# Choosing experts with wider operations, and expert weights in 8 KB pieces

## The chip, the cores and the metric

The kernel runs as one program on one core of a Trainium2 chip. The metric is device time in microseconds (us), the median of three runs. Engines: PE multiplies matrices, DVE and ACT work element by element, POOL (GpSimd) issues the indirect DMAs, SP issues all other DMAs.

## The reference

Two transformer blocks over 512 tokens of 1024 features, all in f32. The change touches only the mixture of experts in the first block. Each token goes to 2 of 32 experts, both from one group of 8:

```
lg = xs @ wr_g + br_g;  pg = softmax(lg);  ptop, gsel = top_k(pg, 1)
le = (xs @ wr_e + br_e) of the chosen group;  lv, esel = top_k(le, 2)
we = softmax(lv) * ptop;  gate = one_hot(gsel) x (we on esel)      # [S, 32]
h = silu(xs @ w_gate[e]) * (xs @ w_up[e]) * gate[:, e];  y = sum over e of h @ w_down[e]
```

An expert has w_gate and w_up of 1024x256 and w_down of 256x1024: three times 1 MB.

## The kernel before

The program is a row of stages. In a stage each engine has its own instruction list, held together by semaphores; a stage ends when all engines are through, and its POOL list begins by clearing the semaphores of the stage before (line 161). `c.settle()` is such a stage with nothing in it but the clearing. Three parts matter here.

**The choice** (`choose`, line 745) works on logits of [128 tokens, 4 row blocks, 36]. DVE runs one chain of small operations, each waiting for the one before (`run`): it finds the best group, masks the experts of the other groups (lines 823 to 828, once per row block), marks the two best experts (`mr`, line 833), and splits the marks into first and second choice (`sel`, `whom`). From `mr`, PE counts how many earlier tokens chose each expert (`ahead`) and how many in all (`total`): 14 matmuls of 32 columns. DVE turns the counts into places (`where`), PE multiplies `where` by `whom` into a list of up to 64 token numbers per expert (line 785), DVE stores it as `table`, and POOL gathers the tokens of experts 0 and 1 by indirect DMA. SP writes the largest count to DRAM. Before the stage ends, the weights of experts 0 and 1 are on their way (`c.to_fetch`, issued by SP as the stage begins).

**Between**: `c.settle()`, then every engine loads the largest count from DRAM into a register and branches; with at most 64 tokens per expert it takes `experts_by_token`.

**The experts** (`experts_by_token`, line 988). Three slots hold raw weights (`wgu`, `wd`); for expert j SP waits until slot j-3 is used up, then issues gate, up and down. The two first are one 256-column half each of `wgu[:, slot, k, 0:512]`. ACT rounds `wgu` in four parts to `w_hi` (line 1130), DVE takes the rest as `w_lo` (line 1171). In one period PE does in this order: gate and up of expert j (lines 1082, 1083: 16 matmuls), the transposes of the tokens of expert j+1 (line 1071, 8), down of expert j-1 (line 1103, 8 passes) and the sums of expert j (line 1091, 8 passes). An f32 matmul shows as two passes in the trace. The token rows `xg` are [64 tokens, 1024 features]; a transpose turns 128 features into partitions, and is the operand that PE loads.

Of the kernel before, what the change touches and what calls it, by code (L numbers as in the profile page):

```python
# [15 lines left out]
F32 = mybir.dt.float32  # L16
# [6 lines left out]
P = 128  # L23
# [721 lines left out]
def choose(c, lg, pair_gates, e, taken, table, most, x_dram, first):  # L745
# [5 lines left out]
    with ExitStack() as ctx:  # L751
        gl, le = c.sb(ctx, "group", [P, NT, 16]), c.sb(ctx, "expert", [P, NT, B])
        top, want, oh, ex = (c.sb(ctx, x, [P, NT, w]) for x, w in (("top", 8), ("want", 8), ("oh", 16), ("ex", 4)))
        mr, s1 = c.sb(ctx, "mr", [P, NT, B]), c.sb(ctx, "first", [P, NT, B])
# [4 lines left out]
        ps = c.ps(ctx, "lists", [P, 512])  # L759
        to_exp, exps, chain, picked, counted, listed, placed, stored = (  # L760
            c.sem(x) for x in ("to_exp", "exps", "dve", "picked", "counted", "listed", "placed", "stored"))
        ahead, total = ps[:, 0:NT * NE].rearrange("p (i e) -> p i e", e=NE), ps[:, NT * NE:NT * NE + NE]
        lists = ps[0:CAP, 256:256 + 2 * NE].rearrange("p (w e) -> p w e", w=2)
        xg, gi, xg_in, indexed = first
        with c.stage() as block:
            @block.sync
            def _(sp):
                sp.wait_ge(placed, 2)
                sp.dma_start(most, most_u[0:1, :]).then_inc(stored, 16)
                sp.wait_ge(stored, 16)  # L770

            @block.tensor
            def _(pe):
                pe.wait_ge(picked, 1)
                for i in range(NT):
                    for j in range(i + 1):
                        pe.matmul(ahead[:, i, :], c.const("before" if j == i else "ones"), mr[:, j, 0:NE],
                                  start=(j == 0), stop=(j == i))
                for i in range(NT):
                    mm = pe.matmul(total, c.const("ones"), mr[:, i, 0:NE], start=(i == 0), stop=(i == NT - 1))  # L780
                mm.then_inc(counted, 1)
                pe.wait_ge(placed, 1)
                for r in range(2):
                    for i in range(NT):
                        mm = pe.matmul(ps[0:CAP, 256:256 + 2 * NE], where[:, r, i, :], whom[:, r, i].rearrange("p w e -> p (w e)"),
                                       start=(r == 0 and i == 0), stop=(r == 1 and i == NT - 1))
                mm.then_inc(listed, 1)
# [9 lines left out]
            @block.gpsimd  # L797
            def _(pool):
                for u in range(2):
                    pool.wait_ge(indexed, u + 1)  # L800
                    pool.indirect_dma_start(out=xg[:, u, :], out_offset=None, in_=x_dram,
                                            in_offset=bass.IndirectOffsetOnAxis(ap=gi[:, u, :], axis=0),
                                            bounds_check=S - 1, oob_is_err=False).then_inc(xg_in[u], 16)

            @block.vector
            def _(dve):
                run = Chain(dve, chain)
                for u in range(2):
                    run(nc.vector.memset(xg[:, u, :], 0.0))
                run(nc.vector.memset(gl[:], NEG))  # L810
# [10 lines left out]
                dve.sem_inc(to_exp, 1)  # L821
                run(nc.vector.tensor_scalar(oh[:, :, 4:8], oh[:, :, 0:4], 1.0, -NEG, ALU.subtract, ALU.mult))
                for i in range(NT):
                    grouped = le[:, i, 0:NE].rearrange("p (g e) -> p g e", e=8)
                    run(nc.vector.tensor_tensor(grouped, lg[:, i, 4:36].rearrange("p (g e) -> p g e", e=8),
                                                oh[:, i, 0:4].unsqueeze(2).broadcast_to([P, 4, 8]), ALU.mult))
                    run(nc.vector.tensor_tensor(grouped, grouped, oh[:, i, 4:8].unsqueeze(2).broadcast_to([P, 4, 8]), ALU.add))
# [5 lines left out]
                run(nc.vector.tensor_scalar(mr[:], mr[:], -NEG / 2, None, ALU.is_ge))  # L833
                dve.sem_inc(picked, 1)
                run(nc.vector.tensor_tensor(e, le[:], top[:, :, 0:1].broadcast_to([P, NT, B]), ALU.subtract))
                run(nc.vector.tensor_tensor(st[:, :, 0:1], top[:, :, 1:2], top[:, :, 0:1], ALU.subtract))
                dve.sem_inc(to_exp, 1)
                run(nc.vector.memset(want[:], 2 * NEG))
# [3 lines left out]
                run(nc.vector.tensor_scalar(sel[:, 0], s1[:, :, 0:NE], -NEG / 2, None, ALU.is_ge))  # L842
                run(nc.vector.tensor_tensor(sel[:, 1], mr[:, :, 0:NE], sel[:, 0], ALU.subtract))
                pairs = c.const("pairs").rearrange("p (r i) -> p r i", r=2)
# [8 lines left out]
                for r in range(2):  # L853
                    for i in range(NT):
                        run(nc.vector.tensor_scalar(where[:, r, i, :], c.const("column"), place[:, r, i:i + 1], None, ALU.is_equal))
                run(nc.vector.tensor_reduce(cnt[:, 0], total, AX.X, ALU.max))
                dve.sem_inc(placed, 1)
                nc.vector.tensor_copy(most_u[:], cnt[:, 0]).then_inc(placed, 1)
                dve.wait_ge(listed, 1)
# [8 lines left out]
                run(nc.vector.tensor_tensor(pair_gates[:, :, 1:2], st[:, :, 1:2], st[:, :, 4:5], ALU.mult))  # L868
                run(nc.vector.tensor_tensor(taken, mr[:], st[:, :, 4:5].broadcast_to([P, NT, B]), ALU.mult))

# [32 lines left out]
def experts(c, x_t, y, gates, w_gate, w_up, w_down, wgu, wd):  # L903
# [3 lines left out]
    with ExitStack() as ctx:  # L907
        wg, wu = (wgu[:, n].rearrange("p k j -> p (k j)").rearrange("p (u k j) -> p u k j", u=2, k=KT) for n in range(2))
        gt = c.sb(ctx, "gt", [P, 2, S])
# [78 lines left out]
def experts_by_token(c, table, x_dram, y_dram, w_gate, w_up, w_down, room_yg, small, wgu, wd, gu_in, d_in, first):  # L988

    nc, U32 = c.nc, mybir.dt.uint32
    SLOTS, PARTS = EXPERT_SLOTS, 4
    xg, gi, xg_in, _ = first
    with ExitStack() as ctx:
# [13 lines left out]
        def part(t, p):  # L1010
            return t[:, 2 * p:2 * p + 2, :]

        with c.stage() as block:
            @block.sync
            def _(sp):
                for j in range(EARLY, NE):
                    s = j % SLOTS
                    if j >= SLOTS:
                        sp.wait_ge(w_split, PARTS * (j - SLOTS) + PARTS)
                    for dst, src in ((wgu[:, s, :, 0:HID], w_gate), (wgu[:, s, :, HID:], w_up)):  # L1020
                        sp.dma_start(dst, src[j].rearrange("(k p) n -> p k n", p=P)).then_inc(gu_in[s], 16)
                    if j >= SLOTS:
# [42 lines left out]
            def _(pe):  # L1065
                def turn_x(j):
                    pe.wait_ge(xg_in[j % 2], 16 * (j // 2) + 16)
                    if j:
                        pe.wait_ge(x_split, j)
                    for k in range(KT):  # L1070
                        mm = pe.transpose(rows_ps[:, k, :], xg[:, j % 2, k * P:(k + 1) * P], c.const("ident", CAP)[:, 0:CAP])
                    mm.then_inc(tx, 1)
# [45 lines left out]
            def _(act):  # L1118
# [6 lines left out]
                def w_round(j, p):  # L1125
                    if j < NE:
                        act.wait_ge(gu_in[j % SLOTS], 32 * (j // SLOTS) + 32)
                        if j:
                            act.wait_ge(used, PARTS * (j - 1) + p + 1)
                        nc.scalar.copy(part(w_hi, p), part(wgu[:, j % SLOTS], p)).then_inc(w_rounded, 1)  # L1130

# [30 lines left out]
            def _(dve):  # L1162
# [1676 lines left out]
def first_block(c, a, y_t, x_rows, lbs, pair, dram):  # L2839
# [4 lines left out]
    with ExitStack() as outer:  # L2844
# [593 lines left out]
```

## Time and profile before

| | us |
|---|---|
| median of the runs | 2459.65 (2458.9 to 2464.27) |
| the profiled execution | 2462.61 |
| its span, first to last instruction | 2460.8 |
| the choice, first to last gather issue | 767.6 to 793.9 |
| the experts, first transpose to last down | 798.7 to 1118.1 |

The rows of the trace give the start of a piece in us from the span's start, its length, engine, line, operation and operands. "x8" says that eight equal instructions stand together; square brackets hold the idle time before it and what ended that.

### The profile page before, as it was taken

The numbers are of one execution on the slowest core, as the hardware profiler recorded it, in microseconds if no ns is written. First come the engines' busy times: TensorE is split into PE (matmuls) and PEld (weight loads), VectorE is DVE, ScalarE is ACT, GpSimd is POOL, SyncE is SP. The second block draws the span as 40 slices with busy tenths as digits, with TensorE's granted clock in tenths as the row PEclk, the third lists the DMA queues.
The fourth block names the chain that finished last, engine by engine and source line by source line (L and its number), as shares of the span: only waits on it lengthen the run. The fifth ranks groups of instructions, "written<-read, shape, count | busy, mean of one in ns | idle before, by whom it ended". The sixth has DMA issues, their size and how long they took to land. (4 is left out here: it accounts for less than half of the span.)

```text
span 2460.8 us, 30153 instructions
## 1 busy us (share of the span) xinstructions
PE 2199.7 (89%) x11250; PEld 1658.7 (67%) x11250; DVE 1359.9 (55%) x2399; ACT 897.2 (36%) x1538; POOL 104.7 (4%) x151
## 2 busy tenths in 40 slices
PE   6898998899995999992799989999979998899997
PEld 4687765566775555551677768888757766788886
DVE  2643447766445655553345585974444456778544
ACT  3420233123232666654333342332333334233323
POOL 0000002100000222220000000000000000000000
PEclk8885999999996999996899999999989999999999
DMA  5221322222324999984332122323413221132313
GB/s 163 86 74 40 105 72 65 68 82 65 106 86 142 323 354 346 345 294 178 97 109 57 57 78 76 105 86 107 142 65 115 79 61 65 57 128 78 101 54 111
DMA packets 276334, 296.46 MB, mean 120 GB/s; under 512 B 48861, under 2 KB 248621, under 8 KB 276153
## 3 DMA queue, kind: packets, MB, share of 16 engines
q1 hardware_dynamic: 271066, 286.09, 36.0%
q0 software_dynamic: 5120, 8.40, 1.1%
q8 instruction: 92, 1.51, 0.2%
q14 instruction: 56, 0.46, 0.1%
HBM read 283.12 MB, written 22.07 MB: 124 GB/s over the span
## 5 line engine op out<-in xcount | busy, mean ns | idle before, releaser
L1551 PE MATMUL acc<-x_hi,w_hi 128*128 128x512 f32 x1432 | 579.9, 405 | 20.3 <-DVE w_lo L1502 16.9
L1552 PE MATMUL acc<-x_lo,w_hi 128*128 128x512 f32 x1432 | 566.7, 396 | 0.0
L1553 PE MATMUL acc<-x_hi,w_lo 128*128 128x512 f32 x1432 | 566.2, 395 | 0.0
L1472 ACT CAST w_hi<-raw 128x1024 fp32r<-128x1024 f32 x179 | 186.9, 1045 | 622.5 <-PE acc L1553 587.2
L1502 DVE TENSOR_TENSOR w_lo<-raw,w_hi 128x1024 fp32r<-128x1024 f32 x174 | 212.8, 1224 | 292.8 <-ACT w_hi L1472 289.5
L1551 PEld LDWEIGHTS acc<-x_hi,w_hi 128*128 128x128 f32 x1432 | 274.5, 192 | 84.6 <-DVE w_lo L1502 18.0
L1553 PEld LDWEIGHTS acc<-x_hi,w_lo 128*128 128x128 f32 x1432 | 273.5, 191 | 60.5
L1552 PEld LDWEIGHTS acc<-x_lo,w_hi 128*128 128x128 f32 x1432 | 274.5, 192 | 58.0 <-issue 2.0
L1171 DVE TENSOR_TENSOR w_lo<-wgu,w_hi 128x1024 fp32r<-128x1024 f32 x128 | 150.9, 1220 | 126.9 <-ACT w_hi L1130 126.9
L1130 ACT CAST w_hi<-wgu 128x1024 fp32r<-128x1024 f32 x128 | 127.9, 1045 | 110.1 <-DMA wgu<-in_moe_w_up 104.8
L1082 PE MATMUL ps<-w_hi,xs 128*128 128x512 f32 x256 | 106.2, 415 | 16.7 <-DVE xs L1165 13.7
L1103 PE MATMUL ps<-wd,y 128*64 128x512 f32 x256 | 116.7, 598 | 0.7 <-DVE y L1187 0.7
L1083 PE MATMUL ps<-w_lo,xs 128*128 128x512 f32 x256 | 102.6, 401 | 0.0
L1689 ACT ACTIVATE probs<-scores,stat 128x256 f32<-128x256 f32 (+3 forms) x96 | 51.8, 540 | 127.0 <-DVE stat L1651 126.8
L1511 DVE SCALAR_TENSOR_TENSOR sg<-sg,br 128x512 f32<-128x512 f32 x112 | 76.4, 682 | 34.9 <-PE br L1740 28.2
L2286 DVE SCALAR_TENSOR_TENSOR y_t<-pad,w,y_t 128x512 f32<-128x512 f32 x120 | 90.1, 751 | 3.4
L1698 ACT COPY probs_t<-t_ps 128x256 f32<-128x256 f32 (+3 forms) x96 | 39.1, 407 | 132.0 <-PE t_ps L1612 132.0
L1738 PE MATMUL br<-y_hi,b_hi 128*128 128x512 f32 x176 | 70.8, 403 | 17.1 <-DVE b_lo L1730 16.9
L1551 PE MATMUL acc<-x_hi,lead_hi 128*128 128x512 f32 x184 | 76.5, 416 | 1.3 <-PEq L157 1.0
L1483 ACT ACTIVATE sg<-acc 128x512 f32<-128x512 f32 x112 | 66.2, 591 | 30.2 <-PE acc L1553 30.2
L1552 PE MATMUL acc<-x_lo,lead_hi 128*128 128x512 f32 x184 | 73.9, 402 | 0.0
L1553 PE MATMUL acc<-x_hi,lead_lo 128*128 128x512 f32 x184 | 73.6, 400 | 0.0
(553 smaller groups left out, 3315.6 us busy)
## 6 DMA issues: line engine op xcount, KB each, us to landing
raw<-in_w_in SPq DMA_DIRECT2D x60, 1024.0 KB, 5.4
raw<-in_w_gate SPq DMA_DIRECT2D x40, 1024.0 KB, 5.5
wgu<-in_moe_w_gate SPq DMA_DIRECT2D x32, 1024.0 KB, 11.4
wgu<-in_moe_w_up SPq DMA_DIRECT2D x32, 1024.0 KB, 14.9
wd<-in_moe_w_down SPq DMA_DIRECT2D x32, 1024.0 KB, 9.4
raw_b<-in_w_branch SPq DMA_DIRECT2D x56, 256.0 KB, 2.7
room<-in_w_out SPq DMA_DIRECT2D x3, 2048.0 KB, 8.2
y_t<-in_w_out SPq DMA_DIRECT2D x3, 2048.0 KB, 10.5
```

The costliest lines, as they stand in the source:

```text
L1082: pe.matmul(ps[:, 0, :], xs[:, u, k, :], w_hi[:, k, :], start=(k == 0), stop=False)
L1083: mm = pe.matmul(ps[:, 0, :], xs[:, u, k, :], w_lo[:, k, :], start=False, stop=(k == KT - 1))
L1103: mm = pe.matmul(ps[0:CAP, 1 + 2 * u + half, :], ht[:, u, m * CAP:(m + 1) * CAP], wd[:, j % SLOTS, m, half * 512:half * 512 + 512], start= ...
L1130: nc.scalar.copy(part(w_hi, p), part(wgu[:, j % SLOTS], p)).then_inc(w_rounded, 1)
L1171: nc.vector.tensor_tensor(part(w_lo, p), part(wgu[:, j % SLOTS], p), part(w_hi, p).bitcast(F32), ALU.subtract).then_inc(w_split, 1)
L1472: self.nc.scalar.copy(self.w_hi[n % 2], self.weights(n)).then_inc(self.rounded, 1)
L1502: eng.tensor_tensor(self.w_lo[n % 2], self.weights(n), self.w_hi[n % 2].bitcast(F32), ALU.subtract).then_inc(self.split, 1)
L1511: self.nc.vector.scalar_tensor_tensor(sg, sg, 1.0, self.br[:], ALU.add, ALU.mult).then_inc(self.mixed, 1)
L1551: pe.matmul(acc, hi, tile.hi[:, k, :], start=(k == 0), stop=False)
L1552: pe.matmul(acc, hi, tile.lo[:, k, :], start=False, stop=False)
L1553: mm = pe.matmul(acc, lo, tile.hi[:, k, :], start=False, stop=(k == KT - 1))
L2286: run(nc.vector.scalar_tensor_tensor(conf[:, m, :], src, wt, conf[:, m, :], ALU.mult, ALU.add))
```

## The change

In `choose`:
- The two memsets of `xg` go from DVE to POOL, as one. `mr` gets a fifth, zero block, set by POOL.
- The masks of lines 825 and 827 are taken over all four row blocks at once; `max` stays one per row block.
- Counts: one matmul with "before" over all five blocks of `mr`, then for each row block j one with "ones", block j repeated into the blocks j+1 and later. Five matmuls of 160, 128, 96, 64 and 32 columns; the fifth block of the result is `total`. `lists` goes to a bank of its own.
- The inputs of the weights' exponentials (`e`, `st`) are computed after `most_u`.
- The eight comparisons to `where` no longer wait for each other, and PE waits for each by itself.

`c.settle()` goes. In `experts_by_token`, `wgu` keeps gate and up apart, and feature p*8+k goes to partition p, block k, instead of feature k*128+p. A partition's share of gate or of up is then 8 KB in one piece on both sides. The transposes take every eighth feature to match.

```diff
@@ choose
-                for i in range(NT):
-                    for j in range(i + 1):
-                        pe.matmul(ahead[:, i, :], c.const("before" if j == i else "ones"), mr[:, j, 0:NE],
-                                  start=(j == 0), stop=(j == i))
-                for i in range(NT):
-                    mm = pe.matmul(total, c.const("ones"), mr[:, i, 0:NE], start=(i == 0), stop=(i == NT - 1))
+                pe.wait_ge(cleared, 1)
+                pe.matmul(counts, c.const("before"), mr[:, :, 0:NE], start=True, stop=False)
+                for j in range(NT):
+                    mm = pe.matmul(counts[:, j + 1:, :], c.const("ones"), mr[:, j:j + 1, 0:NE].broadcast_to([P, NT - j, NE]),
+                                   start=False, stop=(j == NT - 1))
                 mm.then_inc(counted, 1)
-                pe.wait_ge(placed, 1)
                 for r in range(2):
                     for i in range(NT):
+                        pe.wait_ge(placed, r * NT + i + 1)
...
             def _(pool):
+                nc.gpsimd.memset(mr[:, NT, :], 0.0).then_inc(cleared, 1)
+                nc.gpsimd.memset(xg[:, 0:2, :], 0.0).then_inc(cleared, 1)
+                pool.wait_ge(cleared, 2)
...
-                for u in range(2):
-                    run(nc.vector.memset(xg[:, u, :], 0.0))
...
+                run(nc.vector.tensor_tensor(grouped, lg[:, :, 4:36].rearrange("p i (g e) -> p i g e", e=8),
+                                            oh[:, :, 0:4].unsqueeze(3).broadcast_to([P, NT, 4, 8]), ALU.mult))
+                run(nc.vector.tensor_tensor(grouped, grouped, oh[:, :, 4:8].unsqueeze(3).broadcast_to([P, NT, 4, 8]), ALU.add))
...
-                        run(nc.vector.tensor_scalar(where[:, r, i, :], c.const("column"), place[:, r, i:i + 1], None, ALU.is_equal))
+                        nc.vector.tensor_scalar(where[:, r, i, :], c.const("column"), place[:, r, i:i + 1], None, ALU.is_equal
+                                                ).then_inc(placed, 1)
                 run(nc.vector.tensor_reduce(cnt[:, 0], total, AX.X, ALU.max))
-                dve.sem_inc(placed, 1)
-                nc.vector.tensor_copy(most_u[:], cnt[:, 0]).then_inc(placed, 1)
+                nc.vector.tensor_copy(most_u[:], cnt[:, 0]).then_inc(most_ready, 1)
+                run(nc.vector.tensor_tensor(e, le[:], top[:, :, 0:1].broadcast_to([P, NT, B]), ALU.subtract))
+                run(nc.vector.tensor_tensor(st[:, :, 0:1], top[:, :, 1:2], top[:, :, 0:1], ALU.subtract))
+                dve.sem_inc(to_exp, 1)
@@ experts_by_token
-                    for dst, src in ((wgu[:, s, :, 0:HID], w_gate), (wgu[:, s, :, HID:], w_up)):
-                        sp.dma_start(dst, src[j].rearrange("(k p) n -> p k n", p=P)).then_inc(gu_in[s], 16)
+                    for n, w in enumerate((w_gate, w_up)):
+                        sp.dma_start(wgu[:, s, n], w[j].rearrange("(p k) n -> p k n", p=P)).then_inc(gu_in[s], 16)
...
-                        mm = pe.transpose(rows_ps[:, k, :], xg[:, j % 2, k * P:(k + 1) * P], c.const("ident", CAP)[:, 0:CAP])
+                        mm = pe.transpose(rows_ps[:, k, :], xg[:, j % 2, k:D:KT], c.const("ident", CAP)[:, 0:CAP])
...
-                        nc.scalar.copy(part(w_hi, p), part(wgu[:, j % SLOTS], p)).then_inc(w_rounded, 1)
+                        nc.scalar.copy(part(w_hi, p), raw_part(j, p)).then_inc(w_rounded, 1)
@@ first_block
         choose(c, lg[:], pair, e[:], taken[:], table, dram["most"], dram["x"], first)
-        c.settle()
```

PE in the choice, before, from the branch into the stage to the branch out of it:

```order
L772 UNCONDITIONAL_BRANCH
L777 MATMUL lists<-mr,consts 128x32 x10
L780 MATMUL lists<-mr,consts 128x32 x4
L785 MATMUL lists<-whom,where 64x64 x8
L157 UNCONDITIONAL_BRANCH
```

and the same place after:

```order
L773 UNCONDITIONAL_BRANCH
L777 MATMUL lists<-mr,consts 128x160
L779 MATMUL lists<-mr,consts 128x128
L779 MATMUL lists<-mr,consts 128x96
L779 MATMUL lists<-mr,consts 128x64
L779 MATMUL lists<-mr,consts 128x32
L785 MATMUL lists<-whom,where 64x64 x8
L157 UNCONDITIONAL_BRANCH
```

Fourteen count matmuls have become five; the eight for the lists stand as they were. DVE after the marks are made, before:

```order
L835 TENSOR_TENSOR e<-expert,top 128x160
L836 TENSOR_TENSOR st<-top 128x4
L838 MEMSET want 128x32
...
L847 TENSOR_TENSOR whom<-sel,consts 128x4x32 x4
L851 TENSOR_TENSOR t<-lists,sel 128x128 x2
L852 TENSOR_REDUCE place<-t 128x8
L855 TENSOR_SCALAR where<-consts,place 128x64 x8
L856 TENSOR_REDUCE count<-lists 128x1
L858 CAST most_u<-count 128x1
L860 TENSOR_SCALAR table<-lists 64x2x32
```

and after:

```order
L836 MEMSET want 128x32
...
L845 TENSOR_TENSOR whom<-sel,consts 128x4x32 x4
L849 TENSOR_TENSOR t<-lists,sel 128x128 x2
L850 TENSOR_REDUCE place<-t 128x8
L853 TENSOR_SCALAR where<-consts,place 128x64 x8
L855 TENSOR_REDUCE count<-lists 128x1
L856 CAST most_u<-count 128x1
L857 TENSOR_TENSOR e<-expert,top 128x160
L858 TENSOR_TENSOR st<-top 128x4
L861 TENSOR_SCALAR table<-lists 64x2x32
```

Two operations have moved from ahead of `whom` to just ahead of `table`. POOL from the clearing of the stage before the choice to the branch on the largest count, before:

```order
L161 ISA x38
L797 UNCONDITIONAL_BRANCH
L801 DMA y<-x_scratch,gi 64x1024 x2
L157 UNCONDITIONAL_BRANCH
L158 UNCONDITIONAL_BRANCH
L161 ISA x8
L157 UNCONDITIONAL_BRANCH
L2967 TENSOR_LOAD most
```

and after (`y` is the memory that `xg` lies in):

```order
L161 ISA x38
L797 UNCONDITIONAL_BRANCH
L799 MEMSET mr 128x40
L800 MEMSET y 64x2048
L804 DMA y<-x_scratch,gi 64x1024 x2
L157 UNCONDITIONAL_BRANCH
L2970 TENSOR_LOAD most
```

The empty stage with its eight clearings is gone, and two memsets stand ahead of the gathers.

## Rows read from the trace of the kernel before

**Rows 1.** Waits from 848 to 1105 us: waiter, releaser, us in total, times, longest us.

```profile
ACT w_hi L1130 <- DMA wgu<-in_moe_w_up: 101.1, 26, 4.8
...
PE ps L1082 <- DVE xs L1165: 13.4, 26, 0.7
```

**Rows 2.** Stretches: length, busy of PE, PEld, DVE, ACT, POOL, PE clock, DMA share, GB/s.

```profile
811.48:847.84 36.36, 36.08 (x161) 21.68 (x161) 22.22 (x25) 25.47 (x38) 9.22 (x14) 1.00 0.95 310
847.84:1105.27 257.43, 241.04 (x1041) 143.47 (x1041) 141.85 (x157) 156.10 (x236) 58.23 (x102) 0.99 1.03 339
```

**Rows 3.** Timeline of PE among the experts.

```profile
819.53 1.10 PE L1091 MATMUL ps<-consts,y 128*128 128x64 f32 x8
...
824.29 0.71 PE L1071 MATMUL ps<-consts,y 64*128 64x64 f32 x8
824.93 3.65 PE L1103 MATMUL ps<-wd,y 128*64 128x512 f32 x8
...
846.45 1.10 PE L1091 MATMUL ps<-consts,y 128*128 128x64 f32 x8
...
1104.35 1.10 PE L1091 MATMUL ps<-consts,y 128*128 128x64 f32 x8
```

**Rows 4.** The same view as rows 2: DMA alone, in two short stretches.

```profile
772.00:775.00 3.00, 0.00 (x0) 0.00 (x0) 2.47 (x16) 0.21 (x1) 0.00 (x0) 0.50 1.10 355
784.00:786.00 2.00, 0.36 (x2) 0.22 (x2) 1.39 (x5) 0.00 (x0) 0.00 (x0) 0.50 1.04 412
```

**Rows 5.** Timeline of the choice, from the end of the stage before to the first transpose.

```profile
766.89 0.20 DVE L3310 TENSOR_TENSOR logits<-out_ps,rb 128x36 f32<-128x36 f32 x1 [3.22 <-PE out_ps L3245]
...
767.62 0.91 DVE L809 MEMSET y<- 64x1024 f32 x1 [0.54 <-PEq L157]
...
769.80 0.11 DVE L810 MEMSET group<- 128x64 f32 x1
...
773.51 0.19 DVE L825 TENSOR_TENSOR expert<-logits,oh 128x32 f32<-128x32 f32 x1
...
776.30 0.09 DVE L829 MEMSET want<- 128x32 f32 x1
...
778.17 4.48 PE L777 MATMUL lists<-mr,consts 128*128 128x32 f32 x20 [11.32 <-DVEq L834]
778.21 0.33 DVE L835 TENSOR_TENSOR e<-expert,top 128x160 f32<-128x160 f32 x1
...
778.92 0.09 DVE L838 MEMSET want<- 128x32 f32 x1 [0.18 <-DVE st L836]
...
781.02 1.27 DVE L847 TENSOR_TENSOR whom<-sel,consts 128x128 f32<-128x128 f32 x4
...
784.47 0.62 DVE L851 TENSOR_TENSOR t<-lists,sel 128x128 f32<-128x128 f32 x2 [2.18 <-PE lists L780]
...
785.58 2.28 DVE L855 TENSOR_SCALAR where<-consts,place 128x64 f32<-128x64 f32 x8
...
788.20 1.97 PE L785 MATMUL lists<-whom,where 128*64 128x64 f32 x16 [3.84 <-DVEq L857]
...
790.20 0.22 DVE L860 TENSOR_SCALAR table<-lists 64x64 uint32<-64x64 f32 x1 [1.82 <-PE lists L785]
...
792.92 0.95 POOL L801 DMA_INDIRECT y<-x_scratch,gi  x1 [0.30 <-issue]
798.67 1.10 PE L1071 MATMUL ps<-consts,y 64*128 64x64 f32 x8 [8.51 <-PEq L157]
```

**Rows 6.** Groups by line, DVE: mean ns of a 128x128 operation on two tensors.

```profile
L851 DVE TENSOR_TENSOR t<-lists,sel 128x128 f32<-128x128 f32 x2 | 0.6, 292 | 2.2 <-PE lists L780 2.2
```

**Rows 7.** Groups by line, DVE, 512 elements: one operand with a step of 32, and none.

```profile
L454 DVE TENSOR_TENSOR av<-av 128x512 f32<-128x512 f32 x1 | 1.0, 1047 | 0.0
...
L1893 DVE TENSOR_TENSOR sq<-merged 128x512 f32<-128x512 f32 x2 | 1.3, 688 | 0.0
```

**Rows 8.** Groups by line, POOL: a memset.

```profile
L2226 POOL MEMSET pad<- 128x1084 f32 x2 | 2.0, 1006 | 1056.3 <-issue 1056.3
```

More of the change, by code:

```diff
@@ L753, in choose @@
         top, want, oh, ex = (c.sb(ctx, x, [P, NT, w]) for x, w in (("top", 8), ("want", 8), ("oh", 16), ("ex", 4)))
-        mr, s1 = c.sb(ctx, "mr", [P, NT, B]), c.sb(ctx, "first", [P, NT, B])
+        mr, s1 = c.sb(ctx, "mr", [P, NT + 1, B]), c.sb(ctx, "first", [P, NT, B])
         st, cnt = c.sb(ctx, "st", [P, NT, 8]), c.sb(ctx, "count", [P, 2, 1])
@@ L758, in choose @@
         where, most_u = c.sb(ctx, "where", [P, 2, NT, CAP]), c.sb(ctx, "most_u", [P, 1], mybir.dt.uint32)
[L759 to L763, printed above, removed]
+        ps = c.ps(ctx, "lists", [P, 2, 512])
+        to_exp, exps, chain, picked, counted, listed, placed, most_ready, cleared, stored = (
+            c.sem(x) for x in ("to_exp", "exps", "dve", "picked", "counted", "listed", "placed", "most_ready", "cleared", "stored"))
+        counts = ps[:, 0, 0:(NT + 1) * NE].rearrange("p (i e) -> p i e", e=NE)
+        ahead, total = counts[:, 0:NT, :], counts[:, NT, :]
+        lists = ps[0:CAP, 1, 0:2 * NE].rearrange("p (w e) -> p w e", w=2)
         xg, gi, xg_in, indexed = first
@@ L767, in _ @@
             def _(sp):
-                sp.wait_ge(placed, 2)
+                sp.wait_ge(most_ready, 1)
                 sp.dma_start(most, most_u[0:1, :]).then_inc(stored, 16)
@@ L774, in _ @@
                 pe.wait_ge(picked, 1)
-                for i in range(NT):
-                    for j in range(i + 1):
-                        pe.matmul(ahead[:, i, :], c.const("before" if j == i else "ones"), mr[:, j, 0:NE],
-                                  start=(j == 0), stop=(j == i))
-                for i in range(NT):
-                    mm = pe.matmul(total, c.const("ones"), mr[:, i, 0:NE], start=(i == 0), stop=(i == NT - 1))
+                pe.wait_ge(cleared, 1)
[3 more added lines that the diff above has]
+                                   start=False, stop=(j == NT - 1))
                 mm.then_inc(counted, 1)
-                pe.wait_ge(placed, 1)
                 for r in range(2):
                     for i in range(NT):
-                        mm = pe.matmul(ps[0:CAP, 256:256 + 2 * NE], where[:, r, i, :], whom[:, r, i].rearrange("p w e -> p (w e)"),
+                        pe.wait_ge(placed, r * NT + i + 1)
+                        mm = pe.matmul(ps[0:CAP, 1, 0:2 * NE], where[:, r, i, :], whom[:, r, i].rearrange("p w e -> p (w e)"),
                                        start=(r == 0 and i == 0), stop=(r == 1 and i == NT - 1))
@@ L822, in _ @@
                 run(nc.vector.tensor_scalar(oh[:, :, 4:8], oh[:, :, 0:4], 1.0, -NEG, ALU.subtract, ALU.mult))
+                grouped = le[:, :, 0:NE].rearrange("p i (g e) -> p i g e", e=8)
+                run(nc.vector.tensor_tensor(grouped, lg[:, :, 4:36].rearrange("p i (g e) -> p i g e", e=8),
+                                            oh[:, :, 0:4].unsqueeze(3).broadcast_to([P, NT, 4, 8]), ALU.mult))
+                run(nc.vector.tensor_tensor(grouped, grouped, oh[:, :, 4:8].unsqueeze(3).broadcast_to([P, NT, 4, 8]), ALU.add))
                 for i in range(NT):
[L824 to L827, printed above, removed]
                     run(nc.vector.max(top[:, i, :], le[:, i, :]))
@@ L832, in _ @@
                     run(nc.vector.match_replace(mr[:, i, :], want[:, i, :], le[:, i, :], -NEG))
-                run(nc.vector.tensor_scalar(mr[:], mr[:], -NEG / 2, None, ALU.is_ge))
+                run(nc.vector.tensor_scalar(mr[:, 0:NT], mr[:, 0:NT], -NEG / 2, None, ALU.is_ge))
                 dve.sem_inc(picked, 1)
-                run(nc.vector.tensor_tensor(e, le[:], top[:, :, 0:1].broadcast_to([P, NT, B]), ALU.subtract))
-                run(nc.vector.tensor_tensor(st[:, :, 0:1], top[:, :, 1:2], top[:, :, 0:1], ALU.subtract))
-                dve.sem_inc(to_exp, 1)
                 run(nc.vector.memset(want[:], 2 * NEG))
@@ L842, in _ @@
                 run(nc.vector.tensor_scalar(sel[:, 0], s1[:, :, 0:NE], -NEG / 2, None, ALU.is_ge))
-                run(nc.vector.tensor_tensor(sel[:, 1], mr[:, :, 0:NE], sel[:, 0], ALU.subtract))
+                run(nc.vector.tensor_tensor(sel[:, 1], mr[:, 0:NT, 0:NE], sel[:, 0], ALU.subtract))
                 pairs = c.const("pairs").rearrange("p (r i) -> p r i", r=2)
@@ L868, in _ @@
                 run(nc.vector.tensor_tensor(pair_gates[:, :, 1:2], st[:, :, 1:2], st[:, :, 4:5], ALU.mult))
-                run(nc.vector.tensor_tensor(taken, mr[:], st[:, :, 4:5].broadcast_to([P, NT, B]), ALU.mult))
+                run(nc.vector.tensor_tensor(taken, mr[:, 0:NT], st[:, :, 4:5].broadcast_to([P, NT, B]), ALU.mult))
 def gates_to_dram(c, e, taken, gates, gu_in, d_in, xg_in):
@@ L907, in experts @@
     with ExitStack() as ctx:
-        wg, wu = (wgu[:, n].rearrange("p k j -> p (k j)").rearrange("p (u k j) -> p u k j", u=2, k=KT) for n in range(2))
+        wg, wu = (wgu[:, n] for n in range(2))
         gt = c.sb(ctx, "gt", [P, 2, S])
@@ L1010, in part, with raw_part @@
         def part(t, p):
-            return t[:, 2 * p:2 * p + 2, :]
+            return t[:, 2 * p:2 * p + 2, :].rearrange("p k (n j) -> p k n j", n=2)
+        def raw_part(j, p):
+            return wgu[:, j % SLOTS, :, 2 * p:2 * p + 2, :].rearrange("p n k j -> p k n j")
         with c.stage() as block:
@@ L1170, in w_rest @@
                         dve.wait_ge(w_rounded, PARTS * j + p + 1)
-                        nc.vector.tensor_tensor(part(w_lo, p), part(wgu[:, j % SLOTS], p), part(w_hi, p).bitcast(F32),
+                        nc.vector.tensor_tensor(part(w_lo, p), raw_part(j, p), part(w_hi, p).bitcast(F32),
                                                 ALU.subtract).then_inc(w_split, 1)
@@ L2958, in first_block @@
         moe = a["moe_w_gate"][0], a["moe_w_up"][0], a["moe_w_down"][0]
-        wgu, wd = c.sb(ctx, "wgu", [P, EXPERT_SLOTS, KT, 2 * HID]), c.sb(ctx, "wd", [P, EXPERT_SLOTS, 2, D])
+        wgu, wd = c.sb(ctx, "wgu", [P, EXPERT_SLOTS, 2, KT, HID]), c.sb(ctx, "wd", [P, EXPERT_SLOTS, 2, D])
         gu_in, d_in = ([c.held_sem(x) for _ in range(EXPERT_SLOTS)] for x in ("gu_in", "d_in"))
         for n in range(EARLY):
-            c.to_fetch += [(wgu[:, n, :, at:at + HID], w[n].rearrange("(k p) n -> p k n", p=P), gu_in[n])
-                           for at, w in ((0, moe[0]), (HID, moe[1]))]
+            c.to_fetch += [(wgu[:, n, m], w[n].rearrange("(p k) n -> p k n", p=P), gu_in[n]) for m, w in enumerate(moe[0:2])]
             c.to_fetch.append((wd[:, n], moe[2][n].rearrange("(k p) n -> p k n", p=P), d_in[n]))
         choose(c, lg[:], pair, e[:], taken[:], table, dram["most"], dram["x"], first)
-        c.settle()
         most = nc.values_load(dram["most"], min_val=0, max_val=S)
```

## The prediction

> **What bounds the kernel now.** I read the page's slices first: the DMA engines are full in one long stretch only, some 300 us of 2461, and the diff touches that stretch and the 31 us ahead of it. Elsewhere the program is the same, so I cost these two places and nothing else.
>
> The waits among the experts come next [rows 1]. In 26 periods ACT waits 101.1 us for w_up, the second weight transfer, and through ACT and DVE this reaches PE: 13.4 us ahead of gate and up. The stretches [rows 2] show why. From 848 to 1105 us the DMA share is 1.03 at 339 GB/s: transfers are the bound. But from 811 to 848 us PE is busy 36.08 of 36.36 us: at first, with three slots ahead, PE is the bound. Both periods can be read on PE's sums [rows 3]: (846.45 - 819.53) / 3 = 8.97 us while PE is the bound, (1104.35 - 846.45) / 26 = 9.92 us while DMA is. So faster transfers can give back at most 0.95 us a period; then PE decides. That PE is 94% busy in the DMA-bound part (241.04 of 257.43) says the same.
>
> Last the choice [rows 5]: DVE is one chain from 767.62 us on, broken by two waits for PE (t after the counts, 2.18 us; table after the lists, 1.82 us), then come POOL's gathers to 793.87, and then 4.80 us until PE's first transpose. Every us saved on this chain is saved in the end, because nothing else of the experts can begin.
>
> **The choice, part by part.**
> - Memsets of `xg`: DVE began its first other operation at 769.80 instead of 767.62. Saved 2.18 us. On POOL one memset of 64x2048 should last 1.9 us by 1006 ns for 1084 elements [rows 8]; POOL has over 13 us, clearings included, until the gathers, so I cost it at nothing. PE's first count waits for the small memset ahead of it, due 8 us after the stage begins.
> - Masks: the loop took 776.30 - 773.51 = 2.79 us for 12 operations, 0.23 us each. Eight go (1.86 us), two of 128 columns come, at 292 ns [rows 6] and some 30 ns for the chain: 0.65 us. Saved 1.2 us.
> - Counts: `t` began 784.47 - 778.17 = 6.30 us after PE's first count, for 28 passes, 0.224 us each. DVE itself reached the wait at 782.29. Now there are 10 passes. Weight loads alone make 10 x 0.224 = 2.2 us; if the columns came on top in full, at 3.65 us / 8 / 512 = 0.89 ns a column and pass at full clock, twice that at the clock of 0.50 that [rows 4] show here, 480 columns x 2 passes would add 1.7 us: 2.2 to 3.9 us. DVE's own way from the marks to the end of `whom` is now 782.29 - 778.92 = 3.37 us, since `e` and `st` (0.71 us) have left it. So DVE waits little: `t` starts 3.4 to 3.9 us after the first count. Saved 2.4 to 2.9; I take 2.9, since loads and columns overlapped before (0.224 us a pass is no more than the load).
> - Lists: from the first comparison to `table` it was 790.20 - 785.58 = 4.62 us. Now PE starts after one comparison (0.3 us) and needs its 1.97 us: 2.3 us. DVE needs eight comparisons without chain waits, 0.19 to 0.25 us each, then count and cast (0.4) and `e` and `st` (0.6): 2.5 to 3.0 us. Saved 1.6 to 2.1; I take 2.0. The exponentials now end late, but only the tail of DVE needs them, which ended 2 us before POOL.
> - Empty stage: what lies between 793.87 and 798.67 us is a stage's end, eight clearings, the empty stage's end, the register load, the branch, a stage's start. One stage border without clearings took 767.62 - 767.09 = 0.53 us. Bounds 0.5 and 2.0; I take 0.9, the border and its clearings. The clearings are now done in a later stage, in which POOL has nothing else.
>
> Sum: 2.2 + 1.2 + 2.9 + 2.0 + 0.9 = 9.2 us, bounds 7.9 to 10.4.
>
> **The experts.** What pieces are worth is seen where DMA works alone [rows 4]: from 772 to 775 us it moves gate and up, 1 KB a piece, at 355 GB/s; from 784 to 786 us w_down, 4 KB a piece, at 412 GB/s, with every engine full both times. Gate and up are 2.10 MB an expert: 5.91 us at 355, 5.09 us at 412. The 8 KB pieces may do slightly better; no row shows them in bulk, so I take 412. The transfer-bound period is 9.92 - 0.82 = 9.10 us (w_down, gathers and scatters unchanged). PE's is 8.97. Two bounds this close give a period slightly above both: I take 9.20, estimated. From 846.45 on there are 26 periods: 26 x 0.72 = 18.7 us. Bounds: 0 (pieces don't matter) and 26 x 0.95 = 24.7 (PE alone decides). The first five periods were PE's already and stay.
>
> The Trainium skill speaks against this (DMA: Bandwidth & Descriptors, "Where 436 GB/s comes from"): between HBM and SBUF the HBM share of a core, about 358 GB/s, is said to bind. The 412 GB/s of rows 4 is above that, so the trace disagrees here. By the rule the period would be 9.92 x 339 / 358 = 9.39 us and the gain of this part 14 instead of 19 us.
>
> ACT and DVE read the raw parts in runs of 256 elements instead of one of 1024. In the PE-bound stretch [rows 2] ACT is busy 70% and DVE 61%, which hides that and the earlier arrival of the weights.
>
> The transposes are the open cost. Each now loads 128 features with a step of 8 elements, and PE, the next bound, has no cover: it does them in line. Now it takes 0.71 us for eight [rows 3], 0.089 us each. No PE operand of before has a step. The nearest row is DVE's [rows 7]: 512 elements with one operand at a step of 32 take 1047 ns, without one 688, so 0.70 ns more an element; on 128 x 8 elements that is 0.72 us a period, PE's bound 9.69 us and the gain of the part about 4 us. The other end is nothing, if PE's load takes its elements singly anyway. I take nothing, since a transpose's load is short of what 128 elements would cost at DVE's pace (128 x 1.3 = 172 ns), so PE's port is the faster; this choice is my weakest.
>
> The sum: 9.2 + 18.7 = 27.9 us. The profiled execution would go from 2462.6 to 2434.7; the median of the runs, 3.0 us lower, from 2459.65 to 2431.8.
>
> **Rivals.**
> 1. Transfers don't get faster: the engines then carry 339 GB/s whatever the piece, for example because gathers and scatters slow them. Against it rows 4, for it that these show no mix. Only the choice's 9.2 us: 2450.
> 2. The step costs PE what it costs DVE: period 9.69, from the second sum to the last 29 x 9.69 = 281.0 instead of 284.8 us, 3.8 + 9.2 = 13.0 us: 2447.
> 3. Slower: the step costs more. Before, those 29 periods took 284.8 us, and PE's own make 29 x 8.97 = 260.1; with 9.2 us from the choice the point of balance lies at (284.8 + 9.2 - 260.1) / 29 = 1.17 us a period, 0.235 us a transpose instead of 0.089. If a strided load took four times as long, 0.355 us, the period would be 11.1 us and the time 2459.65 + 322 - 284.8 - 9.2 = 2488. Against it: rows 7 make a factor of 1.5 of it on DVE. For it: PE is 99% busy when not held up, so every bit of it shows. The Trainium skill has this as a rule (SBUF — State Buffer, "Door 1: The DMA port swizzle", its note on cachelines): lines are 16 bytes, four f32, and each access to a new line pays. Every element here would be a new line, where four shared one; DVE's rows agree that a long step costs, not that it costs four times.
> 4. The choice gains less than its sum, because a border or the register load grows by what the stages lose (the gathers are waited for instead): 3 to 4 us of the 9. That only shifts the others.
>
> **How the numbers follow.** Forecast, 2424 to 2438: 0.52. Rival 1 with what lies between, 2438 to 2452: 0.20. Rival 2, 2438 to 2455: 0.17. Between that and no change: 0.03. Rival 3: 0.08. The range for 8 in 10 is 2423 to 2452; its low end is PE's bound with the choice's best, 2459.65 - 24.7 - 10.4 = 2424.5, less a little for the spread of runs. A difference under 0.2%, 5 us, can't be told from none. So faster 0.88, same 0.04, slower 0.08.
>
> **What would show it.** Right: gate and up land with a DMA share near or under 1 at 360 GB/s or more; ACT's wait for w_up falls from 101 us to under 30; sums follow each other every 9.0 to 9.3 us; eight transposes still take 0.71 us; `t` starts under 4 us after the first count, `table` about 2.6 us after the first comparison; the first transpose comes near 789.5 us. Wrong: transposes over 1.4 us for eight with PE never waiting (rivals 2, 3), or ACT still waiting some 4 us a period for w_up (rival 1).

## The result, and the profile after

| | before | after |
|---|---|---|
| median of the runs, us | 2459.43 (2458.9 to 2464.27, 4 runs) | 2440.05 (2439.05 to 2443.96, 4 runs) |
| ratio to before | | 0.9904, 95% interval 0.9885 to 0.9923 |
| span of the profiled execution | 2460.8 | 2442.1 |

19.4 us faster by the medians, where 27.9 were forecast; by the ratio it is 0.96% or some 24 us. The spans differ by 18.7, but eight of the fourteen traced executions, after's among them and before's not, run about 5 us late from 126 us of the span on, in a part that is the same in all of them, because the clock granted to PE is 0.50 to 0.56 of full speed there instead of 1.00 (the 128 matmuls of line 577 take 11.46 us in after and 7.14 in before). After's stage before the choice ends at 771.22 instead of 767.09 us. So I compare stretches that begin at the end of that stage. From there to PE's sums of the last expert but one, before took 1104.35 - 767.09 = 337.3 us, after 1086.98 - 771.22 = 315.8: 21.5 us less.

The wait of ACT for w_up among the experts, which answers to rows 1 (waiter, releaser, us in total, times, longest us):

```profile
ACT w_hi L1135 <- DMA wgu<-in_moe_w_up: 32.1, 23, 2.6
```

101.1 us have become 32.1, and PE's wait of 13.4 us for `xs` is gone. The stretch from the fifth sum to the last but one, as in rows 2 (length, busy of PE, PEld, DVE, ACT, POOL, PE clock, DMA share, GB/s):

```profile
843.62:1086.98 243.36, 243.36 (x1042) 150.51 (x1041) 143.47 (x156) 163.74 (x234) 72.82 (x102) 1.00 0.96 356
```

PE is busy for all of 243.36 us: it is the bound now, with DMA at 356 GB/s and a share of 0.96. Its timeline, which answers to rows 3:

```profile
815.54 1.10 PE L1096 MATMUL ps<-consts,y 128*128 128x64 f32 x8
...
820.30 1.09 PE L1076 MATMUL ps<-consts,y 64*128 64x64 f32 x8
...
824.90 1.10 PE L1096 MATMUL ps<-consts,y 128*128 128x64 f32 x8
...
1086.98 1.10 PE L1096 MATMUL ps<-consts,y 128*128 128x64 f32 x8
```

The period is (1086.98 - 815.54) / 29 = 9.36 us, to the hundredth the same every time. It was 8.97 in before's own PE-bound stretch [rows 3]. The difference stands in the second column, the lengths: eight transposes take 1.09 us where they took 0.71. Transfers alone, as in rows 4, now with 8 KB pieces for two thirds of the bytes, in two short stretches and in a long one:

```profile
776.00:778.00 2.00, 0.00 (x0) 0.00 (x0) 1.61 (x8) 0.21 (x1) 0.00 (x0) 0.50 1.02 430
780.00:782.00 2.00, 2.00 (x10) 2.00 (x10) 1.76 (x12) 0.00 (x0) 0.00 (x0) 0.50 1.05 438
774.00:788.00 14.00, 4.42 (x26) 4.10 (x26) 12.05 (x62) 0.65 (x3) 1.78 (x2) 0.50 1.01 417
```

Short stretches reach 430 and 438 GB/s, but others between them 401 to 412 (w_down is still in 4 KB pieces). The mean is 417, against 365 in before from 770 to 784 us, where gate and up came in 1 KB pieces. Last the choice, which answers to rows 5:

```profile
771.02 0.20 DVE L3313 TENSOR_TENSOR logits<-out_ps,rb 128x36 f32<-128x36 f32 x1 [3.22 <-PE out_ps L3248]
...
771.56 0.11 DVE L811 MEMSET group<- 128x64 f32 x1 [0.35 <-PEq L157]
...
773.98 1.80 POOL L800 MEMSET y<- 64x2048 f32 x1
...
774.51 1.32 DVE L820 TENSOR_SCALAR oh<-oh 128x64 f32<-128x64 f32 x1
...
779.91 0.90 PE L777 MATMUL lists<-mr,consts 128*128 128x160 f32 x2 [8.93 <-DVEq L835]
...
782.08 1.27 DVE L845 TENSOR_TENSOR whom<-sel,consts 128x128 f32<-128x128 f32 x4
783.39 0.62 DVE L849 TENSOR_TENSOR t<-lists,sel 128x128 f32<-128x128 f32 x2
...
784.49 1.39 DVE L853 TENSOR_SCALAR where<-consts,place 128x64 f32<-128x64 f32 x8
784.80 1.97 PE L785 MATMUL lists<-whom,where 128*64 128x64 f32 x16 [2.45 <-DVE where L853]
...
786.81 0.22 DVE L861 TENSOR_SCALAR table<-lists 64x64 uint32<-64x64 f32 x1 [0.20 <-PE lists L785]
...
789.69 0.95 POOL L804 DMA_INDIRECT y<-x_scratch,gi  x1 [0.30 <-issue]
794.56 1.13 PE L1076 MATMUL ps<-consts,y 64*128 64x64 f32 x8 [7.78 <-PEq L157]
```

| stretch, us | before | after | forecast saving | saving |
|---|---|---|---|---|
| end of stage to first count | 11.08 | 8.69 | 2.2 + 1.2 | 2.39 |
| first count to `t` | 6.30 | 3.48 | 2.9 | 2.82 |
| `where` to `table` | 4.62 | 2.32 | 2.0 | 2.30 |
| `table` to end of last gather issue | 3.67 | 3.83 | | -0.16 |
| to the first transpose | 4.80 | 3.92 | 0.9 | 0.88 |
| all, end of stage to first transpose | 31.58 | 23.34 | 9.2 | 8.24 |
| first transpose to second sum | 20.86 | 20.98 | | -0.12 |
| second sum to last but one (29 periods) | 284.82 | 271.44 | 18.7 | 13.38 |

(`t` to `where` took 1.1 us both times.) Three rows agree with the forecast to 0.3 us. In the first, one comparison on DVE (line 820, 64 elements) took 1.32 us; in before its like took 0.20. It begins inside POOL's memset of `xg` (773.98 to 775.78) and ends 0.05 us after it.

### The profile page after: what moved, and what is told of

The parts are those of the page before. It is cut to its first block and busy times, and to the rows that moved or that the text cites. A ratio compares the mean times of both kernels' runs of the same rounds, so it can differ in the third digit from the quotient of the medians.

```text
span 2442.1 us, 30103 instructions
## 1 busy us (share of the span) xinstructions
PE 2202.9 (90%) x11232; PEld 1664.2 (68%) x11232; DVE 1360.9 (56%) x2391; ACT 906.1 (37%) x1538; POOL 122.2 (5%) x153
```

## The experiments

My theory after the result: transfers no longer decide, PE does, and the 0.39 us a period between 8.97 and 9.36 are the step in the transposes' loads. Rivals: transfers hold the period at 9.36 and PE's longer transposes only fill a wait; or the gain comes from the new arrangement of `wgu` or the earlier start and not from the pieces.

The first four ran on one chip; before had a median of 2465.61 us there.

### e1: the choice alone, 1 KB pieces

The edits of e1 and of e3 to e12 are against the changed kernel. Where the order of the weights changes, the fetches of experts 0 and 1 ahead of the choice change alike.

```diff
-wgu[:, s, n], w[j].rearrange("(p k) n -> p k n", p=P)
+wgu[:, s, n], w[j].rearrange("(k p) n -> p k n", p=P)
...
-xg[:, j % 2, k:D:KT]
+xg[:, j % 2, k * P:(k + 1) * P]
```

Expected: 

> The changed choice without the 8 KB pieces: w_gate and w_up come in 1 KB pieces again (feature k*128+p, transposes of 128 adjacent features), gate and up still apart in wgu. If the choice alone gives what the trace of the changed kernel shows from the end of the stage before to PE's second sums (52.4 to 44.3 us), the time is 8 us below before, about 2451, and the experts keep their period of 9.9 us with ACT waiting for w_up about 100 us. If instead the gain of the experts needs no larger pieces (the arrangement of wgu, an earlier start), the period falls under 9.7 us and the time under 2446.

Measured: 2456.93 us, ratio 0.9964 (0.995 to 0.9978), 8.7 us less than before. The stretch from the fourth sum to the last but one, 27 periods:

```profile
833.01:1101.00 267.99, 250.07 (x1082) 148.86 (x1081) 145.37 (x162) 160.24 (x242) 60.28 (x106) 0.99 1.04 339
```

Period 9.93 us, 339 GB/s at a share of 1.04; before had 9.92, 339 and 1.03. The choice gives 8 us, the pieces make the rest; the arrangement of `wgu` gives nothing.

### e2: the pieces alone

`choose` and `c.settle()` of before, the rest as changed. Expected: 

> The 8 KB pieces and the stepped transposes with the choice and the empty stage of before. Theory: PE decides at 9.36 us a period, 13.4 us less than before over 29 periods, about 2446; with e1 the two gains add up to that of the whole change (19 to 21 us). Rival: the gains overlap (the earlier start is lost in the experts again), then e1 and e2 together are 3 us or more above the whole.

Measured: 2447.91 us, ratio 0.9926 (0.9903 to 0.995).

```profile
840.97:1093.69 252.72, 252.72 (x1081) 156.29 (x1080) 149.84 (x162) 170.62 (x243) 77.84 (x106) 1.00 0.96 357
```

PE is busy throughout, period 9.36. The ratios of e1 and e2 lose 0.0036 and 0.0074, together 0.0110, the whole change 0.0096 in the first measurement and 0.0091 in e9. The sum is 3 to 5 us more than the whole, which taken alone would meet the rival's sign, but the intervals are as wide. The traces settle it: from the end of the stage before the choice to the last sum but one, e1 takes 1101.00 - 771.24 = 329.8 us and e2 1093.69 - 770.41 = 323.3, that is 7.5 and 14.0 less than before's 337.3; together 21.5, as much as the whole change. The gains add up.

### e3: no step, 8 KB pieces

The result is then wrong, since features and weight rows no longer match; only the time is of use.

```diff
-xg[:, j % 2, k:D:KT]
+xg[:, j % 2, k * P:(k + 1) * P]
```

Expected: 

> The changed kernel, but the transposes take adjacent features; weights still in 8 KB pieces (so features and weight rows don't match: products are of the wrong rows). Theory that the step costs PE 0.39 us a period: eight transposes take 0.71 us again and the period falls to 8.97 us if PE alone decides, to 9.1 us if transfers then decide as predicted; 29 periods x 0.26 to 0.39 = 8 to 11 us under the changed kernel, 2429 to 2432. Rival, transfers decide at 9.36 us already: PE gets gaps, the time stays at 2440.

Measured: 2432.39 us, ratio 0.9869 (0.9848 to 0.989). First the stretch, then the loads and the transposes of that line in the whole program (ns, shortest/middle/longest) here, then those of after:

```profile
832.52:1074.80 242.28, 242.28 (x1082) 145.86 (x1081) 148.04 (x162) 166.61 (x243) 77.14 (x106) 1.00 0.99 373
```

```profile
L1076 PEld LDWEIGHTS ps<-consts,y x256: 134/138/223, 794.1 to 1071.0; 64*128 64x128 f32 x128
L1076 PE MATMUL ps<-consts,y x256: 221/223/359, 794.1 to 1071.1; 64*128 64x64 f32 x128
```

```profile
L1076 PEld LDWEIGHTS ps<-consts,y x256: 182/202/203, 794.5 to 1083.1; 64*128 64x128 f32 x128
L1076 PE MATMUL ps<-consts,y x256: 270/271/363, 794.6 to 1083.2; 64*128 64x64 f32 x128
```

223 ns instead of 271 each, the load itself 138 instead of 202, period 8.97, PE without any gap. So the step costs 8 x 48 ns = 0.38 us of the 0.39 between 9.36 and 8.97. The transfers carry 373 GB/s at a share of 0.99. ACT still waits 46.3 us for w_up in these 27 periods (29.5 in e2), but PE waits for nobody: the rival that transfers hold the period at 9.36 is refuted.

### e4 and e5: pieces of 4 KB and 2 KB, steps of 4 and 2

```diff
-wgu[:, s, n], w[j].rearrange("(p k) n -> p k n", p=P)
+wgu[:, s, n].rearrange("p (h q) n -> p h (q n)", h=2), w[j].rearrange("(h p q) n -> p h (q n)", p=P, h=2)
...
-xg[:, j % 2, k:D:KT]
+xg[:, j % 2, k // 4 * 512 + k % 4:(k // 4 + 1) * 512:4]
```

(e5 with h=4, 256 and 2.) Expected of e4: 

> Feature 512h+4p+q at partition p, block 4h+q: pieces of 4 KB, step of 4 elements (16 bytes) in the transposes. If a step within 16 bytes is free, transposes 0.71 us, period 8.97 to 9.1, time 2429 to 2432. If any step costs the same, transposes 1.09 us, period 9.36, 2440. If 4 KB pieces are clearly slower than 8 KB, ACT waits longer for w_up than in e3 and the period lies above that of e3.

Of e5: 

> Pieces of 2 KB, step of 2 elements (8 bytes) in the transposes. Steps of 4 and 8 elements cost 0.280 and 0.271 us a transpose, against 0.223 without. Theory that what counts is how many of the wanted elements lie in one 16-byte line: two here, so 0.223 again and a period near 8.97, if 2 KB pieces are fast enough. Rival, any step costs: 0.27 us, 9.36.

Measured: e4 2444.36 us, ratio 0.9911 (0.989 to 0.9933); e5 in one run 2439.64, beside 2459.57 for before. The transposes of e4, then of e5, then the stretch of e4:

```profile
L1076 PE MATMUL ps<-consts,y x256: 280/280/376, 794.1 to 1085.0; 64*128 64x64 f32 x128
```

```profile
L1076 PE MATMUL ps<-consts,y x256: 278/280/376, 789.5 to 1080.3; 64*128 64x64 f32 x128
```

```profile
834.22:1088.74 254.52, 254.52 (x1081) 158.35 (x1081) 149.75 (x162) 170.59 (x243) 75.53 (x106) 1.00 0.97 355
```

Both expected ways out failed: steps of 4 and of 2 elements cost 280 ns, more than the step of 8. The period is 9.43 in both, PE without a gap. With e4, transfers in 4 KB pieces are not the bound either, and with e5 not even those in 2 KB: most of the gain of the experts needs only the way from 1 to 2 KB. (Of the 7.5 us between the two traced spans 4.6 lie ahead of the choice.) Ahead of the experts, where transfers run alone, 4 KB pieces do as well as after's 417 GB/s; e5 has 393 there, from 770 to 784 us:

```profile
774.00:788.00 14.00, 4.42 (x26) 4.10 (x26) 12.02 (x61) 0.65 (x3) 1.51 (x2) 0.50 1.03 414
```

### e6: 1 KB pieces with the step

e1's weights, after's transposes. Expected: 

> Pieces of 1 KB as before, but the transposes with a step of 8 (features and weight rows don't match: products are of the wrong rows). If transfers decide with 1 KB pieces, the step's 0.39 us a period is hidden in PE's waits: period 9.9 us as in e1. If PE's work adds to the transfers' instead, 10.3.

Measured, one run: 2452.78 us beside 2459.57.

```profile
828.86:1094.13 265.27, 257.26 (x1081) 158.01 (x1081) 144.70 (x161) 160.37 (x241) 60.48 (x106) 1.00 1.04 342
```

265.27 / 27 = 9.82 us a period, with transposes of 271 ns. Its second to sixth periods, while the slots were still ahead, are 9.36. From the seventh sum on transfers decide, and there it is (1094.13 - 856.94) / 24 = 9.88, beside (1101.00 - 861.85) / 24 = 9.96 in e1: where transfers decide, the step hides in PE's waits. The step became dear only through the pieces.

### e7 and e8: what the transfers could do

Both leave out the products with `w_lo`; e8 has e4's pieces and steps as well.

```diff
-                            pe.matmul(ps[:, 0, :], xs[:, u, k, :], w_hi[:, k, :], start=(k == 0), stop=False)
-                            mm = pe.matmul(ps[:, 0, :], xs[:, u, k, :], w_lo[:, k, :], start=False, stop=(k == KT - 1))
+                            mm = pe.matmul(ps[:, 0, :], xs[:, u, k, :], w_hi[:, k, :], start=(k == 0), stop=(k == KT - 1))
```

Expected of e7 (8 KB): 

> The changed kernel without the eight matmuls with w_lo in each expert (their products are left out of the result), so PE has 1.8 us less to do a period and transfers decide. Period = the bound of the transfers with 8 KB pieces: 9.10 if the prediction's sum was right, but e3 ran at 8.97 with PE never waiting, so under 8.97; at 412 GB/s for all 3.4 MB it would be 8.2.

Of e8 (4 KB): 

> As e7 with pieces of 4 KB. Tells what 8 KB give over 4 KB: nothing if pieces of 4 KB already run at full rate (period as e7), up to 0.3 us if each piece still costs its own time.

Measured, one run each: 2429.97 and 2425.5 us.

```profile
830.58:1073.87 243.29, 217.10 (x866) 121.65 (x865) 145.48 (x163) 160.50 (x243) 63.41 (x106) 0.96 0.98 374
```

```profile
825.62:1069.21 243.59, 218.78 (x865) 122.55 (x864) 146.15 (x163) 161.39 (x244) 63.69 (x106) 0.96 0.99 374
```

With 1.8 us less for PE the mean period is 243.29 / 27 = 9.01 us (8 KB) and 243.59 / 27 = 9.02 (4 KB), DMA share 0.98 and 0.99 at 374 GB/s. PE waits now, and its clock falls to 0.96 in the mean, so a part of single periods (7.5 to 11.3 us) may be PE's. Taken together: the transfers' bound is about 9.0 us, and 4 KB pieces do as well as 8 KB. (e8's time is 4.5 us lower, but its stage before the choice also ends 5.3 us earlier, at 766.60 instead of 771.88 us.) My 8.2 us at 412 GB/s for everything is not reached, and gathers, scatters or waits for free slots may be why; that was not tried apart.

### e9 to e12: a version that keeps both gains

e9 is the changed kernel again. e10 sorts the features of the rows in the stage before, where they are stored:

```diff
+                    nc.gpsimd.tensor_copy(xp[:, i, :].rearrange("p (k c) -> p k c", k=KT),
+                                          room[:, i, :].rearrange("p (c k) -> p k c", k=KT)).then_inc(sorted_in, 1)
...
-                    sp.dma_start(x_dram[i * P:(i + 1) * P, :], room[:, i, :]).then_inc(rows_out, 16)
+                    sp.dma_start(x_dram[i * P:(i + 1) * P, :], xp[:, i, :]).then_inc(rows_out, 16)
...
-xg[:, j % 2, k:D:KT]
+xg[:, j % 2, k * P:(k + 1) * P]
```

e11 clears `xg` on ACT (PE's first count then waits for both clearings), and e12 does both:

```diff
-                pe.wait_ge(cleared, 1)
+                pe.wait_ge(cleared, 2)
...
-                nc.gpsimd.memset(xg[:, 0:2, :], 0.0).then_inc(cleared, 1)
+                nc.scalar.activation(xg[:, 0:2, :].rearrange("p u d -> p (u d)"), c.const("ones", CAP)[:, 0:1].broadcast_to([CAP, 2 * D]), ACT.Copy, scale=0.0).then_inc(cleared, 1)
```

Expected of e9: 

> The changed kernel once more, on the chip and beside the runs of before that the next two are compared with: period 9.36 us, some 19 to 22 us under before.

Of e10: 

> 8 KB pieces without steps on PE: in the stage before the choice POOL copies each block of token rows with its features sorted (feature 8c+k to place 128k+c), SP stores the sorted rows, and the transposes take adjacent elements. Theory that the step is all that keeps PE from 8.97 us: the period is 8.97, 29 x 0.39 = 11 us under the changed kernel, if the four copies end before the 8 us do that the stage goes on after the last row block is ready. Rival: the copies on POOL hold up DVE or the stores and cost what the period gives, or the transfers, near their own bound of 9.0 us, hold the period at 9.1 or more: 5 us or less under.

Of e11: 

> The changed kernel with xg cleared by ACT instead of POOL. In its trace one comparison on DVE took 1.32 us instead of 0.20 while POOL's memset ran. If POOL's memset held it up, that comparison takes 0.20 us again and the way from the end of the stage before to the first count shortens by 1.1 us; if it was something else on DVE, it stays.

Of e12: 

> Sorted rows and the clearing on ACT together. If both hold: about 12 us under the changed kernel.

| | median us | ratio to before (2464.75 us) |
|---|---|---|
| e9, changed kernel | 2440.47 | 0.9909 (0.9888 to 0.993) |
| e10, sorted rows | 2434.29 | 0.9885 (0.9866 to 0.9905) |
| e11, clearing on ACT | 2436.75 (one run) | |
| e12, both | 2428.83 | 0.9862 (0.984 to 0.9884) |

The experts of e10, then of e12:

```profile
828.31:1071.01 242.70, 242.48 (x1082) 146.02 (x1081) 147.56 (x162) 165.71 (x243) 67.16 (x106) 1.00 0.99 372
```

```profile
832.11:1074.39 242.28, 242.28 (x1081) 145.92 (x1080) 147.50 (x162) 166.29 (x242) 71.66 (x106) 1.00 0.99 373
```

Both run at 8.97 us (e10 with one period of 9.40). POOL's copies in the stage before, and DVE beside them, in e10:

```profile
753.57 1.31 PE L3249 MATMUL out_ps<-consts,room 128*128 128x128 f32 x8 [1.23 <-DVE room L3304]
753.57 3.16 POOL L3240 COPY sorted<-room 128x1024 f32<-128x1024 f32 x1 [4.15 <-DVE room L3304]
...
755.03 2.78 DVE L3304 SCALAR_TENSOR_TENSOR room<-room,stat,gains 128x1024 f32<-128x1024 f32 x1
...
757.87 2.05 POOL L3240 COPY sorted<-room 128x1024 f32<-128x1024 f32 x1 [1.14 <-DVE room L3304]
```

The third copy takes 3.16 us, and the DVE operation that starts under it 2.78; its like elsewhere in the stage took 1.28 us. DVE has waits for PE there, and the stores end before the stage does, so nothing of it reaches the end: the stage ends at 766.80 us here and at 766.83 in e11, which has no such copies. In the choice of e11 the conflict with POOL's memset is gone:

```profile
766.63 0.20 DVE L3313 TENSOR_TENSOR logits<-out_ps,rb 128x36 f32<-128x36 f32 x1 [3.22 <-PE out_ps L3248]
...
767.10 1.91 ACT L791 ACTIVATE y<-consts 64x2048 f32<-64x2048 f32 x1 [6.08 <-PEq L157]
...
770.11 0.19 DVE L820 TENSOR_SCALAR oh<-oh 128x64 f32<-128x64 f32 x1
...
774.38 0.90 PE L777 MATMUL lists<-mr,consts 128*128 128x160 f32 x2 [7.79 <-DVEq L835]
...
788.87 1.14 PE L1076 MATMUL ps<-consts,y 64*128 64x64 f32 x8 [7.63 <-PEq L157]
```

The comparison takes 0.19 us (0.20 in e2 and e12, where POOL has no memset either; 1.32 to 1.39 in every traced run that has it), the first count comes 774.38 - 766.83 = 7.55 us after the end of the stage before instead of 8.69, the first transpose 22.04 instead of 23.34. e12's stretch from there to the last sum but one is 1074.39 - 771.20 = 303.2 us, against after's 315.8; its interval lies clear of that of e9. It is the fastest version here that computes everything, 35.9 us under before in the medians and by the ratios 0.5% under the changed kernel (0.9862 / 0.9909 = 0.9953).

## Why the prediction was right, and where it was not

- **The bound and what follows it: right.** Transfers decided at 9.92 us, and with them out of the way PE does: 8.97 without the step (e3), so the 0.95 a period that faster transfers can give back was right. (PE's 94% busy, which was said to agree, leaves only 16.4 / 26 = 0.63 us a period idle.) The transfers' new bound, forecast 9.10, is 9.0 (e7), and not over 8.97 as long as PE asks for no more (e3).
- **"The transposes are the open cost ... I take nothing ... my weakest choice": this step failed.** The step costs 48 ns a transpose, 0.39 us a period (e3). The bounds given for it were 0 and 0.72; PE's bound became 8.97 + 0.39 = 9.36 instead of 8.97, and the period 9.36 instead of the 9.20 put in the sum. That is the forecast's one large miss: 18.7 us forecast for the experts, 13.4 measured. Of the 5.3 missing, 26 x 0.16 = 4.2 are in the periods that transfers decided before. The other 3 x 0.39 = 1.2 are in the three periods after the second sum, of which the forecast said that they were PE's already and stay: they went from 8.97 to 9.36. The argument for nothing, that PE's port is faster than DVE's, shows no more than that contiguous loads are faster. DVE's row [rows 7] had a factor of 1.52 for a long step; PE's transposes in a row go from 0.71 to 1.09 us, a factor of 1.53. That the two agree may be chance: steps of 2 and 4 give 1.17 / 0.71 = 1.65.
- **"The memset on POOL: at nothing": wrong by 1.1 us.** POOL had the time, as said, but its memset held up DVE (e11). The cover was counted on POOL only.
- **Counts, lists, empty stage: right** to 0.3 us each (2.82 for 2.9, 2.30 for 2.0, 0.88 for 0.9), and the masks too (1.15 for 1.2, 1.64 us where they took 2.79). The new wait for counts ended before DVE got there, as the lower bound had it. The comparisons without chain waits take 1.39 / 8 = 0.17 us each, under the 0.19 to 0.25 allowed.
- **The signs named ahead.** `t` 3.48 us after the first count, `table` 2.32 after the first comparison: as said. The first transpose comes 23.3 us after the end of the stage before, 22.4 were said. Missed by a little: ACT's wait for w_up 32.1 us (under 30), 356 GB/s (360 or more), period 9.36 (9.0 to 9.3). Missed plainly: eight transposes in 1.09 us (0.71). The time, 2440, lies in the range of 2423 to 2452 but outside the forecast's own 2424 to 2438.
- **The rivals.** Transfers that don't get faster: refuted, 417 GB/s for 365 where they run alone and 373 for 339 in the mix. The step at DVE's price (9.69): right in kind, nearly double in size. The step at four times a load: refuted. The Trainium skill's rule on 16-byte lines (SBUF — State Buffer, "Door 1: The DMA port swizzle") lets steps up to four f32 go free. PE does not bear it out here: steps of 2 and 4 cost more than 8 (280 ns beside 271). The Trainium skill also has a limit of about 358 GB/s for one core between HBM and SBUF (DMA: Bandwidth & Descriptors, "Where 436 GB/s comes from"). The traces disagree: 373 GB/s in e3's mix, 417 alone. After's own trace, with 356 GB/s and 9.36 us, looks just like what the prediction worked out by that limit (9.39 us, 14 us gained). Only e3 tells that PE made it so; that the numbers meet is chance.
- **The size.** Of the 27.9 us, 5.3 are missing in the experts and 1.0 in the choice; the medians lie 2 us under the stretches' 21.5, inside the spread of the runs (in e9 they give 24.3).

Not settled: why a step of 8 elements costs less than one of 2 or 4, and how far below 9.0 us the transfers could go beside a PE at full clock.

## What to carry to other kernels

Where a second bound lies 10% under the first and the first is lifted, every small cost that the change puts on the second engine is paid in full: price those first, and with a price from the nearest row rather than with nothing. Take no larger pieces than the bound asks for: 2 KB were enough here to leave PE without a gap. Larger DMA pieces can be bought by changing which partition holds which row, but the layout has to be paid for somewhere; pay where an engine waits (here in a copy one stage earlier) and not in the operand of the busiest engine. An operation moved to an idle engine isn't free if a neighbour works at the same time: look at that neighbour's durations too.

## What the runs showed of the hardware

- A weight load of 64 partitions x 128 f32 in a transpose takes longer with a step of 2, 4 or 8 elements. Eight transposes in a row take 0.71 us without a step, 0.089 each, and 1.09 with a step of 8, 0.136 each; the whole durations are 223, 280, 280 and 271 ns for steps of 1, 2, 4 and 8 (e3, e5, e4, after), those of the loads 138, 215, 213 and 202.
- DMA into SBUF with all engines full, over 14 us, w_down always in 4 KB pieces: 365 GB/s with gate and up in 1 KB pieces (before), 393 in 2 KB (e5), 414 in 4 KB (e4), 417 in 8 KB (after; 418 in e12).
- POOL's memset and copies stretch single DVE operations under them: 1.32 us for 0.20, 2.78 for 1.28, and 0.19 with the memset on ACT. Others under the same POOL operation kept their length (`MATCH_REPLACE8` 0.16 us with and without the memset).
